# A hybrid SSD and long-convolution layer: six heads' scaled inputs on ScalarE, and the last transform of the long convolutions as three F32R products

## What is computed

```python
# mixer A (Mamba-2 SSD), per direction and chunk of 128 tokens
chunk_states = einsum("bcsgn,bcsgr,bcsgrp->bcgrpn", bmat, exp(a_tot[:, :, None] - a_cs), xdt)
def carry_step(state, inp):
    s_chunk, a_chunk = inp
    return state * exp(a_chunk)[..., None, None] + s_chunk, state
# mixer B (Hyena), two orders
u_f = rfft(u, n=2 * seqlen, axis=1)
k_f = rfft(k, n=2 * seqlen, axis=0)
return irfft(u_f * k_f[None], n=2 * seqlen, axis=1)[:, :seqlen]
```

## Time and profile before

| | |
|---|---|
| time, median of 3 | 4014.41 us (4010.56 to 4015.59) |
| profiled execution, own time | 4012.46 us |
| its span from first to last instruction | 4010.7 us |
| mean granted TensorE clock | 0.957 of full speed |
| PE, DVE, ACT, POOL busy | 92%, 43%, 30%, 25% of the span |
| long convolutions, about | 2224 us to 2860 us of the span |
| states, about | 2913 us to 3058 us of the span |

### The profile page before, as it was taken

How to read it: one execution, slowest core, us unless ns; L and a number is a source line. 1 busy time by engine, 2 the same in 40 slices (tenths; PEclk the granted TensorE clock), 3 DMA queues, 4 the chain that set the end, 5 groups by cost and what they waited for, 6 DMA issues and landing times. The chain is left out here.

```text
span 4010.7 us, 44395 instructions
## 1 busy us (share of the span) xinstructions
PE 3676.8 (92%) x16946; PEld 2984.5 (74%) x16946; DVE 1705.7 (43%) x2042; ACT 1201.0 (30%) x2339; POOL 982.8 (25%) x465
## 2 busy tenths in 40 slices
PE   6799999999999999996799899999856888799998
PEld 2688888888888888884599677777645777688886
DVE  5544420001434330003644455455376666566662
ACT  3311111111010111112377455554203553333332
POOL 0021112121222221211000100101057554444442
PEclk8899999999999999997899999999788899899998
DMA  7533322121111121217999857856486543655552
GB/s 259 168 105 120 113 86 78 63 78 63 68 73 68 73 79 63 78 52 266 301 300 275 184 126 166 194 129 154 122 302 222 158 145 124 224 188 191 202 194 103
DMA packets 386934, 597.39 MB, mean 149 GB/s; under 512 B 152019, under 2 KB 238979, under 8 KB 374395
## 3 DMA queue, kind: packets, MB, share of 16 engines
q1 hardware_dynamic: 297229, 403.94, 33.4%
q10 hardware_dynamic: 80336, 157.83, 10.3%
q0 software_dynamic: 9216, 33.56, 3.7%
HBM read 392.22 MB, written 203.03 MB: 148 GB/s over the span
## 5 line engine op out<-in xcount | busy, mean ns | idle before, releaser
L579 PE MATMUL pl_bank<-hl_hi,pl_w_hi 128*128 128x512 f32 x2336 | 923.9, 396 | 19.1 <-POOL pl_w_lo L550 19.1
L580 PE MATMUL pl_bank<-hl_lo,pl_w_hi 128*128 128x512 f32 x2336 | 922.7, 395 | 0.0
L581 PE MATMUL pl_bank<-hl_hi,pl_w_lo 128*128 128x512 f32 x2336 | 922.5, 395 | 0.0
L579 PEld LDWEIGHTS pl_bank<-hl_hi,pl_w_hi 128*128 128x128 f32 x2336 | 440.7, 189 | 121.8 <-issue 19.4
L581 PEld LDWEIGHTS pl_bank<-hl_hi,pl_w_lo 128*128 128x128 f32 x2336 | 440.7, 189 | 103.0
L580 PEld LDWEIGHTS pl_bank<-hl_lo,pl_w_hi 128*128 128x128 f32 x2336 | 440.8, 189 | 102.4
L547 POOL TENSOR_TENSOR pl_w_hi<-pl_w,pl_zero 128x1024 fp32r<-128x1024 f32 x73 | 138.1, 1892 | 1280.8 <-PE pl_bank L581 1276.1
L655 DVE TENSOR_SCALAR pl_res<-pl_raw,pl_taps 128x2048 f32<-128x2048 f32 x40 | 85.5, 2139 | 775.3 <-ACT pl_raw L605 775.3
L1760 PE MATMUL mo_bank<-mo_hi,mo_w_hi 128*128 128x512 f32 x768 | 305.5, 398 | 22.9 <-POOL mo_w_lo L1732 18.5
L1732 POOL TENSOR_TENSOR mo_w_lo<-mo_w,mo_w_hi 128x1024 fp32r<-128x1024 f32 x96 | 237.8, 2479 | 278.1 <-ACT mo_w_hi L1803 278.1
L1762 PE MATMUL mo_bank<-mo_hi,mo_w_lo 128*128 128x512 f32 x768 | 300.5, 391 | 0.0
(11 more groups left out here) (205 smaller groups left out, 5725.9 us busy)
## 6 DMA issues: line engine op xcount, KB each, us to landing
conv_spec<-spec_s SPq DMA_DIRECT2D x248, 256.0 KB, 6.3
mo_w<-in_w_br SPq DMA_DIRECT2D x96, 512.0 KB, 3.7
pl_w<-in_w_rec SPq DMA_DIRECT2D x73, 512.0 KB, 3.2
kern_s<-taps_res SPq DMA_DIRECT2D x16, 2048.0 KB, 7.0
spec_xin<-kern_s SPq DMA_DIRECT2D x64, 512.0 KB, 5.5
spec_s<-spec_res ACTq DMA_DIRECT2D x128, 256.0 KB, 4.1
st_xb<-tok_s SPq DMA_DIRECT2D x36, 768.0 KB, 7.3
u_s<-pl_res ACTq DMA_DIRECT2D x24, 1024.0 KB, 3.9
```

The costliest lines, as they stand in the source:

```text
L579: pe.matmul(out, w_hi[:, q, m], h_hi[:, k, r], start=(k == 0), stop=False)
L580: pe.matmul(out, w_hi[:, q, m], h_lo[:, k, r], start=False, stop=False)
L581: mm = pe.matmul(out, w_lo[:, q, m], h_hi[:, k, r], start=False, stop=(k == KT - 1))
```

## The change

In `phase_long_convs` ACT's copy to `turned` now rounds to F32R, and DVE subtracts that from the bank again to get the rest, `turned_lo` (one 128x512 subtraction for each piece). The table `back` is split once in the same way. `last` becomes six F32R products in place of two F32 products: `back_hi` by `turned`, `back_hi` by `turned_lo`, `back_lo` by `turned`, for each of the two parts. PE's waits on the copy (`s_te`) become waits on the subtraction (`s_tl`).

In `phase_states` ACT scales the first six heads of `wx` (six activations of 128x64 for each direction), and DVE the other ten in one instruction. PE waits for both. ACT's activations stand ahead of its store issues in a step.

```diff
@@ phase_long_convs @@
-        turned = ph.sb("turned", [P, 4, 4, 2, NA])
+        turned = ph.sb("turned", [P, 4, 4, 2, NA], F32R)
+        turned_lo = ph.sb("turned_lo", [P, 4, 4, 2, NA], F32R)
+        back_hi, back_lo = ph.sb("back_hi", [P, 2, P], F32R), ph.sb("back_lo", [P, 2, P], F32R)
...
                 if q >= 2:
-                    pe.wait_ge(s_te, n - 1)
+                    pe.wait_ge(s_tl, n - 1)
...
-                pe.wait_ge(s_te, NQ * j + 2 * r + 2)
+                pe.wait_ge(s_tl, NQ * j + 2 * r + 2)
...
-                    mm = pe.matmul(bank[4 + r % 2][:], back[:, part, :],
-                                   turned[:, 2 * r % 4:2 * r % 4 + 2, :, part, :].rearrange("p a g n -> p (a g) n"),
-                                   start=(part == 0), stop=(part == 1))
+                    at = slice(2 * r % 4, 2 * r % 4 + 2)
+                    hi, lo = (b[:, at, :, part, :].rearrange("p a g n -> p (a g) n") for b in (turned, turned_lo))
+                    pe.matmul(bank[4 + r % 2][:], back_hi[:, part, :], hi, start=(part == 0), stop=False)
+                    pe.matmul(bank[4 + r % 2][:], back_hi[:, part, :], lo, start=False, stop=False)
+                    mm = pe.matmul(bank[4 + r % 2][:], back_lo[:, part, :], hi, start=False, stop=(part == 1))
...
+            nc.scalar.activation(back_hi[:], back[:], ACT.Copy).then_inc(s_bh, 1)
...
+            def turned_low(j, q):
+                n = NQ * j + q
+                dve.wait_ge(s_te, n + 1)
+                nc.vector.tensor_tensor(turned_lo[:, q % 4].rearrange("p g a n -> p (g a n)"), bank[2 + q % 2][:],
+                                        turned[:, q % 4].rearrange("p g a n -> p (g a n)").bitcast(F32), ALU.subtract
+                                        ).then_inc(s_tl, 1)
...
+                    if j > 0:
+                        turned_low(j - 1, q)
                     if j > 0 and q % 2 == 1 and q > 1:
                         gate(j - 1, q // 2 - 1)
@@ phase_states @@
+        HA = 6
+        WA = HA * HD
...
                     pe.wait_ge(s_wx[d], s + 1)
+                    pe.wait_ge(s_wa[d], s + 1)
...
+                for d in range(2):
+                    act.wait_ge(s_ld[d][q], 16 * half + 16)
+                    act.wait_ge(s_mm[d], s + 2)
+                    tail = ssd["tail"][:, bass.ds(chunk[d], 1), d, :].rearrange("p a h -> p (a h)")
+                    for h in range(HA):
+                        ins = nc.scalar.activation(wx[:, d, h * HD:(h + 1) * HD], xb[:, q, d, h * HD:(h + 1) * HD], ACT.Copy,
+                                                   scale=tail[:, h:h + 1])
+                    ins.then_inc(s_wa[d], 1)
...
-                    nc.vector.tensor_tensor(wx[:, d, :].rearrange("p (h n) -> p h n", h=HEADS),
-                                            xb[:, q, d, 0:D].rearrange("p (h n) -> p h n", h=HEADS),
...
+                    nc.vector.tensor_tensor(wx[:, d, WA:].rearrange("p (h n) -> p h n", n=HD),
+                                            xb[:, q, d, WA:D].rearrange("p (h n) -> p h n", n=HD),
```

More of the change, by code:

```diff
@@ L905, in phase_long_convs @@
         s_u, s_p, s_v, s_vm = ph.sem("u"), ph.sem("prod"), ph.sem("inv"), ph.sem("inv_out")
+        s_bh, s_bl, s_tl = ph.sem("back_hi"), ph.sem("back_lo"), ph.sem("turned_lo")
         s_t, s_te, s_back, s_gate, s_st = ph.sem("turn"), ph.sem("turned"), ph.sem("back"), ph.sem("gate"), ph.sem("st")
@@ L1007, in last @@
                 n = NR * j + r
-                pe.wait_ge(s_te, NQ * j + 2 * r + 2)
+                pe.wait_ge(s_tl, NQ * j + 2 * r + 2)
+                if n == 0:
+                    pe.wait_ge(s_bl, 1)
                 if n >= 2:
@@ L1031, in inverse @@
                 elif j:
-                    pe.wait_ge(s_te, NQ * j)
+                    pe.wait_ge(s_tl, NQ * j)
                 out = bank[2 + k % 2][:, 0:CB]
@@ L1097, in gate @@
                                         ALU.mult).then_inc(s_gate, 1)
+            def turned_low(j, q):
[4 more added lines that the diff above has]
+                                        ).then_inc(s_tl, 1)
+            dve.wait_ge(s_bh, 1)
+            nc.vector.tensor_tensor(back_lo[:], back[:], back_hi[:].bitcast(F32), ALU.subtract).then_inc(s_bl, 1)
             for j in range(NV + 1):
@@ L1257, in phase_states @@
         s_ld, s_wx, s_mm = [ph.sems(f"ld{d}", 2) for d in range(2)], ph.sems("wx", 2), ph.sems("mm", 2)
+        s_wa = ph.sems("wa", 2)
+        HA = 6
+        WA = HA * HD
         s_fade, s_new = ph.sems("fade", 2), ph.sems("new", 2)
@@ L1336, in body @@
                     dve.wait_ge(s_mm[d], s + 2)
-                    nc.vector.tensor_tensor(wx[:, d, :].rearrange("p (h n) -> p h n", h=HEADS),
-                                            xb[:, q, d, 0:D].rearrange("p (h n) -> p h n", h=HEADS),
-                                            ssd["tail"][:, bass.ds(chunk[d], 1), d, :].rearrange("p a h -> p (a h)")
-                                            [:, :, None].to_broadcast([P, HEADS, HD]), ALU.mult).then_inc(s_wx[d], 1)
+                    nc.vector.tensor_tensor(wx[:, d, WA:].rearrange("p (h n) -> p h n", n=HD),
+                                            xb[:, q, d, WA:D].rearrange("p (h n) -> p h n", n=HD),
+                                            ssd["tail"][:, bass.ds(chunk[d], 1), d, HA:].rearrange("p a h -> p (a h)")
+                                            [:, :, None].to_broadcast([P, HEADS - HA, HD]), ALU.mult).then_inc(s_wx[d], 1)
                 for d in range(2):
```

## The result

| | before | changed |
|---|---|---|
| median of 5 runs | 4010.56 us (4006.55 to 4015.59) | 3987.58 us (3981.02 to 3990.95) |
| ratio | | 0.994 (95%: 0.9929 to 0.9951) |
| profiled execution, span | 4010.7 us | 3985.0 us |

The changed kernel is 23 us faster, against 20 forecast from one execution; the time lies in the range. Where it came from is another matter. I measured the same pieces in both traces: a transform part from DVE's first copy behind `first` to the first `prod`, a plane loop from there to ACT's last copy of `v`, the states from SP's first load to the last `state`.

The account below looks back on a forecast made before the run. PE was taken to bound the convolutions, and step order, then transfers, the states. Gains of 14.8 and 5.3 us, 20 in all, bring 4012.46 to 3992.4; the median's 1.95 more gives 3994 us, range 3983 to 4005.

Parts of the forecast that it names:

- The products of `last`: Long convolutions: six F32R products at 0.232 us take 1.39 us in place of 1.72, 0.33 less for each `last`.
- The subtraction: Long convolutions: DVE's subtraction of a bank and an SBUF tile takes 0.69 us, about 0.67 in a row of work.
- Rivals C and D: Slower subtraction: C loses most convolution gain, 4006 to 4012 us, chance 0.09; D makes DVE the bound, about 4041, chance 0.06.
- A transform part gains 6 x 0.33 - 0.05: Long convolutions: six rounds save 0.33 us each, the last round's savings go into a new wait; 1.9 us a part.
- 1 to 3 us may be lost: Long convolutions: DVE, with 0.18 us of slack in a round, recovers slowly from three gate waits, losing 1 to 3 us.
- my lower bound of 9: Long convolutions: lower end of the predicted gain, 9 us, where 14.8 was forecast and 21 was the upper bound.
- If a share of 1.0 is the end, the same work needs 95% of the time: States phase: transfers at DMA share 0.95 limit the gain to 5.3 us, steps of 7.3 us in place of 7.73.
- rival A: States phase: transfers don't bind, so the phase gains 12 us and the kernel takes 3987 us; chance 0.18.
- the engines' 6.48: States phase: two `wx` each 0.40 us shorter in the engines' chain bring a plain step from 7.28 to 6.48 us.
- The Trainium skill's two rates: States phase: HBM limit of about 358 GB/s gives steps of at least 7.3 us, about 425 for a lone core 6.2.
- ACT covered by POOL's `faded`: States phase: ACT's six activations, 1.8 us, finish before DVE's second `wx`, which stands behind POOL's `faded`.

Follow-up runs that it names:

- short load: Changed kernel with only columns 512 to 1535 of each `xb` load loaded, and `wx` scaled from them; 3987.64 us, 0.9949 of the kernel before.
- half of `faded`: Changed kernel with POOL scaling 8 of 16 heads and both halves of the new state adding those; 3989.98 us, 0.9940 of the kernel before.

## Why the prediction was right, and which steps weren't

- **The products of `last`**: right. Six rows 0.23 us apart, the round 3.99 us from one `last` to the next as worked out, and eight waits for `turned_lo` of 0.6 to 0.7 us.
- **The subtraction**: right, 691 ns. Rivals C and D had no ground.
- **"A transform part gains 6 x 0.33 - 0.05"**: mis-sized, 1.41 for 1.9. The end of the last round costs 0.33 us and not 0.05, as DVE's second subtraction ends later than at +4.62; and from the first `first` to the first `last` it is now 5.48 us in place of 5.25, since DVE's 3.12 us of copies and subtractions for two pieces (1.74 + 1.38) exceed PE's 2.60. I had checked DVE against PE only in a full round. 1.98 - 0.23 - 0.33 = 1.42; with the final part 11.3 us.
- **"1 to 3 us may be lost" in DVE's recovery**: a loss there is, in other places: the four loops with extra loads are 4.6 us longer in the profiled executions. Six executions of the changed code gave 185.5 to 187.9 us for them, two of the old code 181.2 and 185.4. With so few of the old one, about 3 us given back is likely and not shown; why, stays open. A part that is 1.4 us shorter leaves the loads issued at a loop's end less time to drain before the next loop, which was only argued. The convolutions alone were timed at 9.2 us, just above my lower bound of 9; the phase itself is 7.3 to 7.9 us shorter, which is below it.
- **"If a share of 1.0 is the end, the same work needs 95% of the time"**: the step that failed. The DMA share of 0.95 was no measure of how near the limit was. The short load shows that bytes don't set the step, and the same queues moved 385 to 405 GB/s over 13 steps with 8 and 10 heads on ACT, at shares of 1.00 and 1.01. What I had as rival A was so, and the engines' 6.48 was right to the hundredth for a plain step. 13 steps took 0.91 us less each (7.73 to 6.82), more than the 0.80 of the chain; three of them ran partly at the lower clock, where before it was seven (0.94 of full speed in the mean for 0.88).
- **The Trainium skill's two rates**: the measurement decides for the second. The Trainium skill's DMA: Bandwidth & Descriptors (Where 436 GB/s comes from) has about 358 GB/s as binding between HBM and SBUF, which the 403 GB/s with 10 heads on ACT refute for a core alone. The Trainium skill's HBM Reference (Specifications) gives about 425 for a core alone, and the 403 GB/s, like the 419 of the loads alone, stay under that. What two cores get at once, no run here shows.
- **ACT covered by POOL's `faded`**: right. In a step PE never waits for it. The one wait on it, 10.0 us, is that for the phase's first load; there ACT's six activations (1.54 us) and DVE's `wx` (1.30) both start at 2909.01, so some 0.2 us of it is ACT's own.

The time came out within 7 us of the forecast by luck: an overestimate of 7 us in the convolutions and an underestimate of 9 in the states offset each other. The total alone would have confirmed both. Rival A's 3987 us was met too, and by luck as well: it has the right mechanism in the states with 12 us for 14.6, but the same 14.8 us for the convolutions.

## What to carry to other kernels

A DMA share near 1 doesn't tell whether transfers limit: in the states a fifth of the bytes could go at 1.00 and nothing changed, in plane loop 3 more bytes at 1.00 cost time. Work out the engines' chain and compare the rate with the highest that the same trace shows for the same kind of transfer, or change the bytes and look; and check in the trace that the edit changed the bytes of the stretch that it was meant for. When one engine has little slack in the full round, check the rounds at both ends of a loop too, where its partner has less to do. And when a step alternates between a short and a long form, find what sets the long form before shortening the short one, and count how many there are of each.

## What the hardware showed that I had not expected

- **A lower clock can take back what a shorter step gains.** PE is busy 4 of 6.48 us in a plain step. The granted clock is 1.00 (2.4 GHz) over most steps and falls to a mean of 0.77 over some, where it is at its lower level (1.2 GHz) for part of the step. With plain steps of 6.48 us three of 13 are such, with 6.22 (8 heads on ACT) six, with 5.77 (half of `faded`) eight, and in both of the latter the mean step came out as before. But it is no rule that shorter steps bring more of them: with 5.95 (10 heads) it is three again, and the step gained 0.3 us, and with the 7.28 of the kernel before it is seven. PE stands about 2 us for `wx` ahead of its products in plain and long steps alike. In which steps the clock falls, I can't tell.
- **Three loads in a row on one queue hold up another queue's.** With three gate loads of 512 KB issued in a row, DVE waited 8.6 us for a 256 KB load of spectra in the middle of a loop, and PE with it; spread over loop 7 the same three cost 5.3 us less. Where a loop's DMA share is 0.98 to 1.00 already (loops 0, 3 and 4), spreading them into it cost 6 to 8 us.
- **A DMA share of about 1 goes with very different rates.** Mixed loads and stores reach 403 GB/s from one core at a share of 1.01 in the states, and 340 GB/s at 0.95 with a slower consumer. In plane loop 3 a share of 1.00 goes with 213 GB/s; there the loads of `x` and gate inputs come in pieces of 256 bytes (64 samples of F32), and whether that is the reason no run shows.
